# The third part of the weight rests moves from GpSimd to VectorE in the feed-forward stages

## The reference, cut to what matters

```python
def swiglu(h, w_up, w_down):
    gate, up = jnp.split(h @ w_up, 2, axis=-1)
    return (jax.nn.silu(gate) * up) @ w_down
...
x = x + 0.5 * swiglu(rmsnorm(x, n1), wu1, wd1)
```

## Time and profile before

| what | value |
|---|---|
| median of 3 runs | 2357.43 us (2351.32 to 2357.58) |
| the profiled execution's own time | 2355.15 us |
| its span, from the first to the last instruction | 2353.4 us |
| TensorE clock granted, mean over the span | 0.934 of full speed |
| PE busy | 2106.5 us, 90% |
| DVE busy | 1496.8 us, 64% |
| ACT busy | 1080.9 us, 46% |
| POOL busy | 452.6 us, 19% |

### The profile page before, as it was taken

How to read it: one execution, slowest core, us unless ns; L and a number is a source line. 1 busy time by engine, 2 the same in 40 slices (tenths; PEclk the granted TensorE clock), 3 DMA queues, 4 the chain that set the end, 5 groups by cost and what they waited for, 6 DMA issues and landing times.

```text
span 2353.4 us, 36888 instructions
## 1 busy us (share of the span) xinstructions
PE 2106.5 (90%) x14422; PEld 1984.6 (84%) x14422; DVE 1496.8 (64%) x1958; ACT 1080.9 (46%) x1567; POOL 452.6 (19%) x187
## 2 busy tenths in 40 slices
PE   6999987999999995899895887999986799999997
PEld 6998977899899894899794887899885798898886
DVE  4555876555555656555657435555576578888887
ACT  4334533444433434433443113444445367677775
POOL 2222212222222220222220222222230000000000
PEclk9999989999999997999997887999998789999999
DMA  8554411455455450455541002455450368888885
GB/s 309 188 187 154 151 54 55 164 189 191 152 189 188 159 188 0 153 188 188 177 149 39 1 1 91 158 190 188 153 208 8 124 243 304 311 305 298 308 306 197
DMA packets 73264, 400.57 MB, mean 170 GB/s; under 512 B 8240, under 2 KB 8368, under 8 KB 41136
## 3 DMA queue, kind: packets, MB, share of 16 engines
q1 hardware_dynamic: 72704, 397.22, 49.3%
q10 hardware_dynamic: 432, 1.57, 0.2%
HBM read 397.71 MB, written 1.05 MB: 169 GB/s over the span
## 4 chain that ended last, share of the span: by engine, by line
PE 83%; DVE 11%; ACT 3%; issue 2%; POOL 0%; DMA 0%; DVEq 0%; SPq 0%; PEld 0%; ACTq 0%; PEldq 0%
PE psum L283 24%; PE psum L284 23%; PE psum L285 23%; DVE w_lo L267 2%; PE psum L686 2%; PE psum L694 1%; PE psum L2115 1%; PE psum L699 1%; PE psum L327 1%; DVE hT_lo L348 1%; ACT O L297 1%; PE psum L2128 1%; DVE O L929 1%; DVE O L343 1%; ACT w_hi L260 0%
## 5 line engine op out<-in xcount | busy, mean ns | idle before, releaser
L267 DVE TENSOR_TENSOR w_lo<-ring,w_hi 128x1024 fp32r<-128x1024 f32 x496 | 764.2, 1567 | 390.7 <-ACT w_hi L260 390.1
L260 ACT ACTIVATE w_hi<-ring 128x1024 fp32r<-128x1024 f32 x744 | 743.5, 1050 | 396.3 <-PE psum L285 252.8
L273 POOL TENSOR_TENSOR w_lo<-ring,w_hi 128x1024 fp32r<-128x1024 f32 x160 | 404.5, 2528 | 1194.9 <-ACT w_hi L260 1194.9
L283 PE MATMUL psum<-hT_hi,w_hi 128*128 128x256 f32 x2096 | 592.0, 282 | 23.8 <-DVE hT_lo L348 17.1
L284 PE MATMUL psum<-hT_lo,w_hi 128*128 128x256 f32 x2096 | 590.7, 282 | 0.0
L285 PE MATMUL psum<-hT_hi,w_lo 128*128 128x256 f32 x2096 | 590.3, 282 | 0.0
L283 PEld LDWEIGHTS psum<-hT_hi,w_hi 128*128 128x128 f32 x2096 | 399.9, 191 | 30.5 <-issue 23.7
L283 PE MATMUL psum<-w_hi,hT_hi 128*128 128x256 f32 (+1 forms) x1216 | 388.2, 319 | 38.2 <-issue 22.3
L284 PEld LDWEIGHTS psum<-hT_lo,w_hi 128*128 128x128 f32 x2096 | 399.9, 191 | 3.9
L285 PEld LDWEIGHTS psum<-hT_hi,w_lo 128*128 128x128 f32 x2096 | 400.0, 191 | 0.0
L285 PE MATMUL psum<-w_hi,hT_lo 128*128 128x256 f32 (+1 forms) x1216 | 375.9, 309 | 0.0
(11 more groups left out here) (442 smaller groups left out, 2051.3 us busy)
## 6 DMA issues: line engine op xcount, KB each, us to landing
ring<-in_stream SPq DMA_DIRECT2D x248, 1024.0 KB, 5.3
ring<-in_stream SPq DMA_DIRECT2D x248, 512.0 KB, 4.3
tables<-in_tables SPq DMA_DIRECT2D x1, 2517.0 KB, 20.1
gain_row<-in_gains ACTq DMA_DIRECT2D x3, 512.0 KB, 3.7
rows<-in_rows SPq DMA_DIRECT2D x1, 1288.0 KB, 23.0
X<-in_x SPq DMA_DIRECT2D x1, 1024.0 KB, 4.9
result<-X SPq DMA_DIRECT2D x2, 512.0 KB, 2.7
columns<-in_columns SPq DMA_DIRECT2D x1, 993.0 KB, 14.6
```

What stands on the lines that cost most here:

```text
L260: act.activation(part(w_hi, g, i), ring[:, k, i * PART:(i + 1) * PART], ACT.Copy) \
L267: dve.tensor_tensor(part(w_lo, g, i), ring[:, k, i * PART:(i + 1) * PART], part(w_hi, g, i).bitcast(F32), ALU.subtract) \
L273: pool.tensor_tensor(part(w_lo, g, 2), ring[:, k, 2 * PART:STEP], part(w_hi, g, 2).bitcast(F32), ALU.subtract) \
L283: pe.matmul(out_, w[0], x[0], start=first, stop=False, skip_group_check=True)
```

## The change

The five feed-forward stages no longer have a POOL program. DVE makes the third part of `w_lo` itself, as the last instruction of each step, behind `act_lo`. `split_lo_last` is the same helper as before, called with another engine. In the mixers POOL goes on with the third part. Two waits are new, since both engines now count the same semaphore: DVE waits at the start of a feed-forward stage until POOL's last part is done, and POOL at the start of a mixer until DVE's last part is done.

```diff
-        def ffn_pool(pool, at):
-            n, g0 = STEPS[NETWORK[at][0]], first_step[at]
-
-            def step(s, sv):
-                if g0 + s + 1 < moe_first:
-                    split_lo_last(pool, g0 + s + 1, g0 + sv + 1)
-
-            step(0, 0)
-            step(1, 1)
-            ffn_loop(pool, n, step)
-
...
                 dve.tensor_tensor(act_lo[:, s % 2, :], gated[:, s % 2, :], act_hi[:, s % 2, :].bitcast(F32), ALU.subtract) \
                    .then_inc(ffn_act_ready, 1)
-
+                if g0 + s + 1 < moe_first:
+                    split_lo_last(dve, g0 + s + 1, g0 + sv + 1)
+
+            dve.wait_ge(lo_last_ready, g0 + 1)
             step(0, 0)
             step(1, 1)
             ffn_loop(dve, n, step)
...
                 if kind in MIXERS:
+                    pool.wait_ge(lo_last_ready, first_step[at] + 1)
                     MIXERS[kind]["pool"](pool, at)
-                elif kind == "ffn":
-                    ffn_pool(pool, at)
```

## The result

| | before | after |
|---|---|---|
| median | 2356.47 us (6 runs, 2351.32 to 2357.58) | 2362.61 us (6 runs, 2361.36 to 2364.26) |
| ratio to before, 95% interval | | 1.0029 [1.0017, 1.0041] |
| span of the profiled execution | 2353.4 us | 2359.6 us |
| TensorE clock granted, mean | 0.934 | 0.931 |

The change costs 6.1 us, 0.29%, and the interval leaves out no change at all. The forecast was 2362.6 us.

The account below looks back on a forecast made before the run. TensorE alone was taken to bound the feed-forward steps. Terms of 0 us in steps and stage starts and 5 x 1.04 = +5.2 us at the ends, on 2357.43, gave 2362.6 us, range 2354 to 2369 us.

Parts of the forecast that it names:

- TensorE bounds the steps, term 0: Inside steady feed-forward steps: TensorE is busy 185.00 of 185 us, so moving the third part to DVE costs 0 us.
- The cover of 3.3 us: In a step: DVE's first two parts would end 3.3 us before TensorE's next `up` wants them, 2.3 us before.
- The start of a stage, term 0: At a stage's start: the new waits cost nothing and the third part fits a 2.94 us DVE gap, 0 us.
- The ends, 1.04 us each: At five feed-forward stage ends: the third part on DVE delays the additions, on the chain, by 1.04 us each.
- The sum: Whole kernel: +5.2 us from the five ends, so a median of 2362.6 us, 0.22% more.
- The clock rivals: Behind stage ends: clock falls more often, 2367.4 to 2369.8 us (0.17); clock better or additions hidden, 2355.4 to 2357.8 (0.18).
- at once: Behind the third stage end: the granted clock is 1.00 at once, nothing lost.
- The relief of DVE: In 100 steps: rival that 1.4 us of DVE's blocked time each comes back, up to 140 us, 2217 us (0.03).

Follow-up runs that it names:

- experiment 4: The changed kernel with one spare 128x2048 subtraction on DVE in every step but the last of each feed-forward stage: 2362.25 us.
- experiment 5: The changed kernel with two spare 128x2048 subtractions on DVE in every step but the last of each feed-forward stage: 2441.04 us.
- experiments 1 and 2: 1: the changed kernel with each feed-forward stage's last third part on POOL, 2357.20 us; 2: the kernel before with only those five on DVE, 2362.59 us.
- experiment 3: The changed kernel with one spare 128x2048 subtraction on DVE ahead of the third part in each feed-forward stage's last step: 2370.63 us.

## Why the prediction was right

- **TensorE bounds the steps, term 0.** Right: same period, TensorE 185.00 of 185 us, and experiment 4 adds 230 us of DVE work in the steps for nothing. The cover of 3.3 us was 3.5 us (68.42 to 71.92); in experiment 5 it is used up.
- **The start of a stage, term 0.** Right: the running account does not move there.
- **The ends, 1.04 us each.** Right in place and mechanism, shown by experiments 1 and 2 from both sides and by 3 in its size. A small miss: 0.93 us each. The third part starts at 206.82 and not at 206.86, and the additions start 1.15 us behind it and not 1.2. One sentence of the working was wrong and did no harm by luck: that ACT has nothing else to do meanwhile. Before the change it was busy until 208.30, and X was ready at 208.32. Had its own work ended later, that much of the delay would have been hidden. Nor did the four additions run without a gap: before, there are 0.07 us of waiting in their middle, which is why they take 2.65 us and now 2.48 us.
- **The sum.** 5 x 0.93 = 4.7 us, where I had 5.2. The forecast of 2362.6 us against 2362.61 is therefore partly luck: the last 1.5 us between the spans lie outside the mechanism, most of them in matmuls of the rwkv mixer at a lower clock, and the six runs give a median of before 1.0 us lower than the three that I had.
- **The clock rivals.** At the ends a worse clock is not seen. The first end lost less at 1.2 GHz than before, the fifth gave back 1.4 us, and the matmuls behind the third again lost nothing (the prediction's "at once" holds for them alone; from 814 to 816 us before, while the transposes ran, the clock was 0.50). The Trainium skill (TensorE: Matmul & The Clock Gate, "What's actually happening") has idleness throttle the clock. The trace agrees in that 1.2 GHz follows idle time of TensorE, but a longer idle time did not bring more of it: with 2.68, 3.61 and 5.80 us of idle time at the first end, the matmuls behind the transposes ran at 1.2 GHz for 5.2, 2.9 and 5.4 us (before, the change, experiment 3).
- **The relief of DVE.** Right to be priced at nothing in the feed-forward stages. The Trainium skill (SBUF — State Buffer, "SBUF: two separate sides") has the one of the two engines that starts first hold the shared ports for its whole instruction. The trace agrees: pairs of 3.73 us behind POOL's part, 2.35 us alone. What I did not ask is where in this kernel TensorE does wait for w_lo. The list of waits answers it: its matmuls wait 9.7 us, all in the mixers, which the change leaves out. There the same edit is worth 14 us.

## What to carry to other kernels

Before moving work off a slow engine, look for who waits for its product, stage by stage: here 105 moved instructions were worth nothing, five cost 5 to 6 us, and the same move in the other stages, where TensorE waited for the parts, gained 14 us. In a loop that hides an instruction, look at the last turn by itself, because what stands behind it there is no longer the next turn but the epilogue. And relief of an engine counts only if it makes the thing complete earlier that is waited for: taking the contention away by ordering the two engines one behind the other left the time as it was.

## What the runs showed of the hardware

POOL's subtraction beside DVE's stretches both: in the mixers up to 3.45 us for POOL (2.38 alone) and 4.6 us for DVE's pair (2.35 alone). Against a DVE instruction that reads PSUM and one tensor of SBUF next to nothing is lost: one of the four additions takes 0.69 us beside POOL's part and 0.68 us without it (medians of 20). Each DVE instruction starts about 0.08 us ahead of the listed end of the one before, so a full engine is priced by the distance of starts (1.14 us for 128x1024, 2.26 for 128x2048). And parts of the kernel that no edit touches take some us more or less from one kernel to the next, the rwkv mixer -4.3 to +3.2 us. The granted clock differs there (0.81 and 0.79 above); whether the shift of a stage's end brings that about is not shown, since executions of the same kernel also differ by 5 us with the clock (0.937 and 0.932).
